# Rows of experts handled one by one, and shared out by new weights

## What is computed

```python
def chunk(xc):                                            # 128 tokens
    q = (xc @ w_query).reshape(c, 8, 2, 64)
    scores = jnp.einsum('chpd,hpnd->chpn', q, sub_keys)   # 8 heads, 2 halves, 128 keys
    s1, i1 = lax.top_k(scores[:, :, 0], 16)
    s2, i2 = lax.top_k(scores[:, :, 1], 16)
    cand_s = (s1[..., :, None] + s2[..., None, :]).reshape(c, 8, 256)
    cand_id = (i1[..., :, None] * 128 + i2[..., None, :]).reshape(c, 8, 256)
    top_s, top_j = lax.top_k(cand_s, 16)
    ids = jnp.take_along_axis(cand_id, top_j, axis=-1)
    gate = jax.nn.softmax(top_s, axis=-1)
    u = expert_u[ids]
    pre = jnp.einsum('chkd,cd->chk', u, xc)
    act = gate * jax.nn.gelu(pre, approximate=False)
    return jnp.einsum('chk,chkd->cd', act, expert_v[ids])
```

## Time and profile before

| | us |
|---|---|
| median of 3 runs | 1773.37 |
| lowest, highest run | 1773.05, 1779.76 |
| the profiled execution: span from first to last instruction | 1769.8 |
| the time of a run outside that span (median less span) | 3.6 |

### The profile page before, as it was taken

One profiled execution on the slowest core, in us unless ns is written; L12 is line 12 of the kernel. 1 busy time (PEld: TensorE's weight loads), 2 busy tenths in 40 slices (PEclk: granted clock), 3 DMA queues, 4 the chain that ended last, 5 costly groups with the idle time before them and its releaser, 6 DMA issues.

```text
span 1769.8 us, 13794 instructions
## 1 busy us (share of the span) xinstructions
PE 1402.4 (79%) x4300; PEld 710.9 (40%) x4300; DVE 1063.0 (60%) x2683; ACT 441.2 (25%) x1406; POOL 587.8 (33%) x516
## 2 busy tenths in 40 slices
PE   7985579987669886899578896889867788877777
PEld 6662245453224453446223363445422333333332
DVE  3569855568975535565996533666698454454444
ACT  0412244121222224421212213431212221222222
POOL 0012334433343333434333331344243344344430
PEclk9987889999779998899888998899988989788989
DMA  8347988999889997899989997899988999989992
GB/s 336 120 158 311 372 329 324 420 378 390 323 342 403 398 418 308 332 415 418 398 331 361 377 416 306 332 378 410 418 354 321 379 376 399 409 346 418 394 381 119
DMA packets 94405, 624.41 MB, mean 353 GB/s; under 512 B 10112, under 2 KB 10624, under 8 KB 28800
## 3 DMA queue, kind: packets, MB, share of 16 engines
q0 software_dynamic: 73728, 536.90, 75.9%
q1 hardware_dynamic: 20608, 86.68, 12.5%
HBM read 622.49 MB, written 1.05 MB: 352 GB/s over the span
## 4 chain that ended last, share of the span: by engine, by line
PE 42%; DVE 25%; DMA 22%; ACT 7%; issue 3%; POOL 2%; ACTq 0%; DVEq 0%; POOLq 0%
PE acc L493 29%; DMA ring<-in_rows,ids 22%; DVE ring L988 10%; PE bank L737 2%; ACT act_w L813 2%; PE bank L786 2%; PE bank L527 2%; POOL ring L468 2%; DVE wb L1258 1%; ACT diag L818 1%; PE bank L645 1%; PE bank L532 1%; ACT L810 1%; DVE top_i L1265 1%; DVE top_i L1256 1%
## 5 line engine op out<-in xcount | busy, mean ns | idle before, releaser
L493 PE MATMUL acc<-ring,diag 128*128 128x512 f32 x2048 | 1010.9, 651 | 327.0 <-ACT diag L818 326.9
L468 POOL DMA_INDIRECT ring<-in_rows,ids x512 | 587.6, 1148 | 1139.5 <-PE acc L493 981.0
L988 DVE CUSTOM_DVE_ANT_0 ring<-ring,xc 128x1024 f32<-128x1024 f32 x512 | 613.2, 1223 | 436.3 <-DMA ring<-in_rows,ids 434.6
L493 PEld LDWEIGHTS acc<-ring,diag 128*128 128x128 f32 x2048 | 419.1, 210 | 891.8 <-issue 497.4
L810 ACT ACTIVATE gel<-pre 128x4 f32<-128x4 f32 (+1 forms) x134 | 27.5, 205 | 966.7 <-DVE pre L988 966.5
L818 ACT ACTIVATE diag<-cst,act_w 128x128 f32<-128x128 f32 x512 | 164.3, 390 | 4.4
L813 ACT ACTIVATE act_w<-gate,gel 128x1 f32<-128x1 f32 (+1 forms) x512 | 109.6, 283 | 6.0
L645 PE MATMUL bank<-wring,hT 128*128 128x512 f32 x128 | 56.7, 593 | 0.8 <-DVE hT L1211 0.8
L786 PE MATMUL bank<-wring,hT 128*128 128x512 f32 x128 | 56.5, 593 | 0.3 <-DVE hT L1025 0.3
L810 ACT ACT_TABLE_LOAD x20 | 25.7, 1283 | 115.4 <-DVE pre L988 115.4
L737 PEld LDWEIGHTS bank<-hT,wring 128*128 128x128 f32 x384 | 44.0, 192 | 2.4 <-issue 2.4
(11 more groups left out here) (234 smaller groups left out, 1000.1 us busy)
## 6 DMA issues: line engine op xcount, KB each, us to landing
wring<-in_w_out SPq DMA_DIRECT2D x16, 1024.0 KB, 12.1
wring<-in_w_gate SPq DMA_DIRECT2D x16, 1024.0 KB, 11.6
wring<-in_w_in SPq DMA_DIRECT2D x16, 978.0 KB, 8.7
wring<-in_w_query SPq DMA_DIRECT2D x12, 1024.0 KB, 11.4
ring<-in_rows,ids POOLq DMA_INDIRECT x512, 9.3
ring<-in_w_in SPq DMA_DIRECT2D x8, 978.0 KB, 14.8
wring<-in_w_ple SPq DMA_DIRECT2D x4, 1024.0 KB, 11.3
wring<-in_w_latent SPq DMA_DIRECT2D x4, 768.0 KB, 10.3
```

The source lines that it names most:

```text
L468: pool.indirect_dma_start(out=ring[:, n % RING, :], out_offset=None, in_=rows, in_offset=bass.IndirectOffsetOnAxis(ap=ids[:, w % 2, k:k + ...
L493: last = pe.matmul(acc[:, c, :], diag[:, j, :], ring[:, j, D + c * 512:D + c * 512 + 512], start=False, stop=True, skip_group_check=True)
L988: dve.tensor_tensor_reduce(out=u, in0=u, in1=xc[:, step % 2, :], scale=1.0, scalar=0.0, op0=ALU.mult, op1=ALU.add, accum_out=pre[:, j:j + ...
```

## The change

Every row is handled singly by all engines: `GROUP`, `GROUPS`, `SINGLY`, `share_out` and the loops go, and `Shares` hands out 128 rows a step in place of 32 groups. `choose` gets six turns instead of two; `top16` takes `turn` and calls it after its first `max_index`. The weights of the turns are new. ScalarE's `choose` calls four turns, then waits for the gates' values and takes the exponential, then two turns; TensorE's calls six. The ring stays at 8 slots, the gathers, their order and their waits stay as they are.

```diff
-RING, GROUP = 8, 4
-GROUPS = PAIRS // GROUP
-SINGLY = 2
+RING = 8
...
-FRONT = [1] + [.5] * KT
-LEAVE = [1]
-REST = [1, 1, 1, 1, 1, 1, 1, 1] + [.5] * (KT // 2) + [1] + [.5] * (KT // 2) + [1]
-CHOOSE = [1, 1]
-EMBED = [1] + [.5] * 4
+SLAB = 2.4
+FRONT = [5] + [SLAB] * KT
+LEAVE = [5]
+REST = [2.5, 2.5, 4, 2, 2.5, 1, 1, 5] + [SLAB] * (KT // 2) + [5] + [SLAB] * (KT // 2) + [3]
+CHOOSE = [2.3] * 6
+EMBED = [3] + [SLAB] * 4
...
-        return turns + (FRONT + LEAVE if w >= 1 else []) + REST + CHOOSE * CHUNKS + [1]
-    return turns + [.5, .5, 3]
+        return turns + (FRONT + LEAVE if w >= 1 else []) + REST + CHOOSE * CHUNKS + [2]
+    return turns + [2, 2, 96]
...
-        a, b = self.sent, round(GROUPS * sum(self.turns[:self.n]) / sum(self.turns))
+        a, b = self.sent, round(PAIRS * sum(self.turns[:self.n]) / sum(self.turns))
...
     def __call__(self, step, a, b):
-        share_out(self, step, a, b)
+        for k in range(a, b):
+            self.body(step, k)
...
+            def experts(step, k):                          # TensorE
+                n = step * PAIRS + k
+                j = n % RING
+                pe.wait_ge(diag_ready, n + 1)
+                for c in range(2):
+                    last = pe.matmul(acc[:, c, :], diag[:, j, :], ring[:, j, D + c * 512:D + c * 512 + 512],
+                                     start=False, stop=True, skip_group_check=True)
+                last.then_inc(row_used, 1)
...
+            def experts(step, k):                          # ScalarE
+                n = step * PAIRS + k
+                j = n % RING
+                act.wait_ge(dotted, n + 1)
+                act.activation(gel[:, j:j + 1], pre[:, j:j + 1], ACT.Gelu).then_inc(gelued, 1)
+                act.wait_ge(gelued, n + 1)
+                act.activation(act_w[:, j:j + 1], gate[:, step % 2, k:k + 1], ACT.Copy,
+                               scale=gel[:, j:j + 1]).then_inc(weighted, 1)
+                act.wait_ge(weighted, n + 1)
+                act.activation(diag[:, j, :], ident, ACT.Copy, scale=act_w[:, j:j + 1]).then_inc(diag_ready, 1)
...
+            def experts(step, k):                          # VectorE
+                n = step * PAIRS + k
+                j = n % RING
+                dve.wait_ge(row_in[j], (n // RING + 1) * 16)
+                u = ring[:, j, 0:D]
+                dve.tensor_tensor_reduce(out=u, in0=u, in1=xc[:, step % 2, :], scale=1.0, scalar=0.0,
+                                         op0=ALU.mult, op1=ALU.add, accum_out=pre[:, j:j + 1]).then_inc(dotted, 1)
...
-            def top16(lists, values, indices, data, spare):
+            def top16(lists, values, indices, data, spare, turn):
...
                 for i in lists:
-                    dve.max_index(out=indices[:, i, 0:8], in_max=values[:, i, 0:8], in_values=data(i))
+                    ins = dve.max_index(out=indices[:, i, 0:8], in_max=values[:, i, 0:8], in_values=data(i))
+                turn()
                 for i in lists:
                     ins = dve.match_replace(out=spare(i), in_to_replace=values[:, i, 0:8], in_values=data(i),
...
-                top16(range(2 * h0, 2 * (h0 + n)), top_v, top_i, score, lambda i: wb[:, i * P:(i + 1) * P])
+                top16(range(2 * h0, 2 * (h0 + n)), top_v, top_i, score, lambda i: wb[:, i * P:(i + 1) * P], turn)
+                turn()
...
-                if s == 0:
-                    turn()
                 top16(range(h0, h0 + n), best_v, best_i, lambda i: wa[:, i * 256:(i + 1) * 256],
-                      lambda i: wb[:, i * 256:(i + 1) * 256])
-                if s > 0:
-                    turn()
+                      lambda i: wb[:, i * 256:(i + 1) * 256], turn)
+                turn()
...
                 link(ins)
+                turn()
                 for half in range(2):
                     ins = dve.tensor_tensor(w4[half], w4[half], names[:, :, half, :].unsqueeze(2).broadcast_to(full),
                                             ALU.mult)
```

More of the change, by code:

```diff
@@ L115, in __call__, with __init__ @@
         assert self.n <= len(self.turns)
-        a, b = self.sent, round(GROUPS * sum(self.turns[:self.n]) / sum(self.turns))
+        a, b = self.sent, round(PAIRS * sum(self.turns[:self.n]) / sum(self.turns))
         self.sent = b
[L118 to L136, removed]
-class Stream:
[L142 to L154, removed]
+        self.stream(self.step, a, b)
+class Stream:
+    def __init__(self, body):
+        self.body = body
     def __call__(self, step, a, b):
-        share_out(self, step, a, b)
+        for k in range(a, b):
+            self.body(step, k)
 def walk(stream, parts):
@@ L487, in release @@
                 last.then_inc(weight_used, 1)
[L489 to L495, removed]
+            def experts(step, k):
[6 more added lines that the diff above has]
+                last.then_inc(row_used, 1)
             def begin(w):
@@ L794, in embed @@
                             turn()
-            walk(Stream(pe, experts), {"front": front, "leave": leave, "rest": rest, "choose": choose, "embed": embed, "lift": lift,
+            walk(Stream(experts), {"front": front, "leave": leave, "rest": rest, "choose": choose, "embed": embed, "lift": lift,
                                        "begin": begin, "finish": lambda t: None, "ahead": ahead})
@@ L969, in embed @@
                                    scale=inv[:, 1, 0:1]).then_inc(sig_ready, 1)
[L971 removed]
+            walk(GatedStream(experts), {"front": front, "leave": leave, "rest": rest, "choose": choose, "embed": embed, "lift": lambda s: None,
                           "begin": begin, "finish": lambda t: None, "ahead": ahead})
@@ L982, in link @@
                 next_of(dve_done)
-            def experts(step, i, half, unit=GROUP):
-                for j in range(half * GROUP, half * GROUP + GROUP):
-                    dve.wait_ge(row_in[j], (step * (PAIRS // RING) + i + 1) * 16)
-                    u = ring[:, j, 0:D]
-                    dve.tensor_tensor_reduce(out=u, in0=u, in1=xc[:, step % 2, :], scale=1.0, scalar=0.0,
-                                             op0=ALU.mult, op1=ALU.add, accum_out=pre[:, j:j + 1]).then_inc(dotted, 1)
+            def experts(step, k):
[5 more added lines that the diff above has]
+                                         op0=ALU.mult, op1=ALU.add, accum_out=pre[:, j:j + 1]).then_inc(dotted, 1)
             def rsqrt(sizes, done=dve_done):
```

32 lines of the change are left out of this document (9 added, 23 removed).

## The result

The changed kernel takes 1647.5 us (median of 4 runs, 1642.4 to 1649.7) against 1776.6 of the kernel before beside it: ratio 0.927, 95% interval 0.925 to 0.930. The forecast was 1699 with a range of 1640 to 1760. The profiled execution took 1648.2 us, its span is 1646.3, 123.5 us less than before. Single executions of a kernel can fall into a slower state with a lower granted clock or be disturbed (one of e12 took 1853.7 us, one of e1 4875.2); every median and ratio in this document leaves such executions out.

What follows compares the result with a forecast made beforehand. The prediction took the gather to bound the kernel, starved in attention and choice because ring slots wait for groups of four. Windows 0 to 3 gave -12, -18, -19 and -25, together -74: 1773.4 becomes 1699 us, range 1640 to 1760.

Steps and rivals of the forecast that it cites:

- A single row is paced by its transfer alone: Last rows of the last window, already single: 2.47 us apart, 425 GB/s, against 2.70 us a row in fours.
- the first stretch gets 36 rows instead of 26 ... +20: Window 0's start, with three choice chunks: more rows there lengthen it from 68 to 88 us of VectorE.
- 330 to 408 ... stay: Stretch of window 0 from 330 to 408 us: no change in length expected.
- Window 1: Forecast -18 us: attention -32, choice +18, embedding and front -4.
- The choice: Choice of experts: VectorE 119 us, transfers 130 us, so 112 becomes 130; +18 in window 1, +17 in window 2.
- The attention's chain: Attention: each of 14 rows less saves 1.76 us of a serial chain, 24.6 us, plus 7 of waits; 115 becomes 83.
- The longer program: Straight code instead of loops: fetching it taken as 0, with 5 us either way as a bound.
- Fully fed: Rival: the attention gives back its whole emptiness too; -133, 1640 us; chance 0.12.
- Transfers at their limit: Rival: 341 to 353 GB/s is what memory gives in these mixes, so no gain; 1773 us; chance 0.08.
- Rows left the wrong stage: Rival: attention's length doesn't depend on rows, gives back 5 us a window while choices grow; +36, 1809 us; chance 0.09.
- The clock: Rival: in the choices, TensorE's lower clock makes all 186 rows take 3.44 us; +77, 1850 us; chance 0.03.
- The signs: Last-window rows 2.5 us apart; choice 400 GB/s or more, some 130 us; attention 75 to 90 us under 350 GB/s; choice clock over 0.9.

Runs made afterwards that it cites:

- e12: Changed kernel with rows dealt in multiples of four and ScalarE waiting for the dot product three rows later, both at once: 1798.1 us, ratio 1.011.
- e1: Changed kernel with rows still singly, but the places, two turns in the choice and weights of the kernel before: 1667.8 us, ratio 0.937.
- e9: Changed kernel, rows singly, but ScalarE takes up a row only when the dot product three rows later is there: 1690.5 us, ratio 0.954.
- e10: Changed kernel with single rows but old places, two turns and old weights, run again for its trace: 1668.9 us by its timed runs.
- e4: Changed kernel with the attention's eight weights raised from 20.5 to 35, 28 rows there in place of 18: 1630.5 us, ratio 0.916.

## Why the prediction was right, and where its sizes were off

**The bound and its cause** were right: the gather was short of slots because a group holds them, 13 us against 4.5. "A single row is paced by its transfer alone" held for the last window (2.49 us), and I had read it off the eight last rows. Two things in the cause were coarser than the traces. The wait for the other rows is the largest part of the hold, but by itself it would have cost the stream little (e9). And TensorE doesn't wait for all four diagonals, as I had written: it starts behind the first, 1644.46 - 1642.80 = 1.66 us after the GELU, not 2.49.

```profile
1644.46 7.13 PE L493 MATMUL acc<-ring,diag 128*128 128x512 f32 x16 [2.31 <-ACT diag L818]
```

**The sum** was -74 us on the span and -123.5 came. By window, from `begin` to `begin`: -12 forecast and -46 measured; -18 and -32; -19 and -25; -25 and -21. So two thirds of the miss is one window.

*Window 0.* The step that failed is "the first stretch gets 36 rows instead of 26 ... +20". The trace has 32 dot products before the attention's first own instruction and 38 after, of which 8 and 10 lie ahead of 158 us: four rows more, not ten. I had also set the whole stage's VectorE time (88 us) against the part of it behind 158. Measured from 158: 76 us before and 71 after, -6. The second term is "330 to 408 ... stay": between the squares of `y` and the first maximum it went from 88 to 69 us, -19. Its attention gave 21 where I had 36, and the last choice grew by 0.5 us where I had 4.

*Window 1.* Attention -37.5 (forecast -32), choice +13.0 (+18), embedding and front -4.9 (-4), projections -2.3 (0): each within 6 us. *Window 2:* attention -24 (-32), choice +9.5 (+17), front -5.7 (-4), projections -4.4 (0).

*The choice* is VectorE's, as worked out. Two chunks begin at

```profile
784.70 0.89 DVE L1223 MAX8 top_v<-bank 128x8 f32<-128x128 f32 x4
...
814.58 0.89 DVE L1223 MAX8 top_v<-bank 128x8 f32<-128x128 f32 x4
```

29.9 us apart with twelve rows, where the earlier trace rows had 24.6 with eight: 15.4 + 12 x 1.15 = 29.2.

*The attention's chain* was taken at 1.76 us a row; going from 18 rows to 28 measured 1.6, and singly with 32 rows (e10) against 18 (changed) it is 99.7 to 73.8 us for 14 rows, 1.85 a row. I had 25 us of the 32 from fewer rows and 7 from single ones; e10 and the changed kernel split the measured 37.5 into 26 and 11.5. The 26 are largely paid back where the rows went.

*The split of the change*, and the term that was too small. The prediction made no claim of how much each part brings, and its terms for the choices hold both, more rows and being fed. The runs say: singly 6.3%, six turns 0.3, weights 0.7, and places without single rows lose 3.2%. By window, e10 is 33, 24, 21 and 21 us shorter than the kernel before, and the changed kernel another 13, 8 and 4 us shorter, and 1 us longer in the last. So single rows alone gave 77 us outside the last window, where my whole sum, places and all, had 49. That is the mis-sized term: single rows feed every stage that starved, and I had priced this stage by stage too low, at 7 us for window 1's attention (11.5 in e10) and at nothing between window 0's attention and choice (88 us before, 77 in e10).

*ScalarE.* Forecast +203 us with the gaps inside its chain; +154 us of busy time came (441.2 to 595.6). In the stream it is hidden, since every row still waits for the DMA.

*The longer program*, which I had put at nothing without a row to show it: the two instruction queues moved 0.91 MB against 0.82, which at 420 GB/s is 0.2 us.

**The rivals.** *Fully fed* gave 1640 and is nearer in time than the forecast, but not what happened: 36 us of the attentions stay empty. Its price was also added up wrongly: the midpoint of 74 and 175 is 124.5, not 133, so it should have read 1649 us, and the measured 1647.5 would have met it, but by luck. *Transfers at their limit* fell: 422 GB/s for 264 us. *Rows left the wrong stage* holds in its direction: e4, with ten rows given back, is 17 us faster. It was priced as a loss against the kernel before, which it isn't, because the attention's length does follow its rows. *The clock* rose instead. With six turns a chunk the pauses in the choice stay short,

```profile
789.03 3.70 PE L465 MATMUL acc<-ring,diag 128*128 128x512 f32 x8 [0.58 <-ACT diag L785]
795.00 3.70 PE L465 MATMUL acc<-ring,diag 128*128 128x512 f32 x8 [2.27 <-ACT diag L785]
```

and the granted clock is 0.97 there. In e10, with two turns a chunk, eight rows took 16.98 us after a pause of 7.85, and the clock stood at 0.83:

```profile
829.74 16.98 PE L464 MATMUL acc<-ring,diag 128*128 128x512 f32 x32 [7.85 <-ACT diag L784]
```

In the changed kernel such a burst is left after a long pause in the attention:

```profile
616.19 8.52 PE L465 MATMUL acc<-ring,diag 128*128 128x512 f32 x16 [7.40 <-ACT diag L785]
```

8.52 us for 16, like the 8.55 of the earlier trace rows. The Trainium skill (TensorE: Matmul & The Clock Gate, "A second HAM failure mode: psum-queue depth-cycling") warns that a matmul stream with frequent short idle times can swing between the two clock levels. The stream of single rows doesn't show it: with a pause of 0.5 us in front of each row it ran at 1.00 over 264 us. The clock can't be the main cause of the gain: e10 has the choice at 0.83, as before, and most of the gain.

**The signs** named in the prediction came: rows 2.5 us apart, the choice at 421 GB/s and 133 us long with VectorE 90% busy, a clock over 0.9 there. The attention is 74 and 90 us long as named, but window 1's runs at 369 GB/s, above the 350 I had given it.

## What to carry to other kernels

Where a ring feeds on what its last consumer releases, measure how long a slot is held, from its first use to the issue of the next transfer into it. That hold and the time from issue to landing have to fit into the number of slots times the transfer of one; here 4.5 us left much room and 13 us none. Handling elements singly can then be worth more than the batch saves, as long as each engine's single step is shorter than a transfer.

Then deal the elements out so that no stage of the other work is without them, and try the dealing in both directions: a long chain between engines takes more of them than its own busy time suggests (here 28 of 128 rather than 18). When forecasting, give every stage whose transfers aren't at the full rate its own term for the change, and cut a stage at the trace's own marks.

## What the runs showed of the hardware

The transfers reach 421 to 423 GB/s in slices of 41 us, and 422 over 264 us at a share of 1.01, on one core. The median time from a gather's issue to its landing is 14.3 us, against 9.3 before, while more bytes moved a second (379 GB/s in the mean against 353): the transfers were not slower, they stood in line. TensorE's granted clock was 1.00 in the stream, with 1.98 us of its work in every 2.49 us.
